# Three double-width projections, a list read later, and a program with two ends, in a hybrid encoder layer with mixture of experts

## The reference, cut to what matters

```python
proj = h @ w_in            # q 256 | k 256 | v 512 | og 512 | a1 16 | z 512 | xbc 1024 | dt 8
o_gla = rms_norm(gla_chunk_causal(q, k, v, log_a)) * silu(og)
y     = rms_norm((ssd_chunk_causal(xs, dt, a, bm, cm) + xs * ssd_d) * silu(z))
h = layer_norm(alpha * h + concat(o_gla, y) @ w_out)
top_v, top_i = lax.top_k(h @ router_w + router_b, 4); gates = softmax(top_v)   # of 32 experts
for each expert e, on the tokens that chose it:
    out += gate * ((min(a, 7) * sigmoid(1.702 * a) * (clip(u, -7, 7) + 1)) @ w_down[e] + b_down[e])
    # a = x @ w_gate[e] + b_gate[e],  u = x @ w_up[e] + b_up[e]
return layer_norm(alpha * h + out)
```

## Time and profile before

| what | value |
|---|---|
| median of three runs | 1058.77 us |
| the profiled execution | 1058.86 us |
| its span, first to last instruction | 1057.0 us |
| TensorE matmuls busy | 1021.6 us, 97% |
| TensorE weight loads busy | 449.5 us, 43% |
| VectorE, ScalarE, GpSimd busy | 228.6, 143.9, 29.7 us |
| moved by the DMAs | 426.21 MB, 403 GB/s over the span |

### The profile page before, as it was taken

How to read it: one execution, slowest core, us unless ns; L and a number is a source line. 1 busy time by engine, 2 the same in 40 slices (tenths; PEclk the granted TensorE clock), 3 DMA queues, 4 the chain that set the end, 5 groups by cost and what they waited for, 6 DMA issues and landing times.

```text
span 1057.0 us, 12137 instructions
## 1 busy us (share of the span) xinstructions
PE 1021.6 (97%) x5116; PEld 449.5 (43%) x5116; DVE 228.6 (22%) x495; ACT 143.9 (14%) x348; POOL 29.7 (3%) x50
## 2 busy tenths in 40 slices
PE   8999999999999999999999999999999999999997
PEld 7888764333333333333333333333333333333332
DVE  5453572111111111111111112211111111111112
ACT  3312331111111111011110111111111110011102
POOL 1230100000000000000000000000000000000000
PEclk9999999999999999999999999999999999999999
DMA  9894689999999999999999999999999999999995
GB/s 314 273 410 192 201 327 410 428 428 435 429 429 435 432 425 433 435 436 424 430 435 436 424 422 436 432 430 426 435 434 428 428 435 435 430 425 427 428 418 236
DMA packets 40011, 426.21 MB, mean 403 GB/s; under 512 B 6922, under 2 KB 19347, under 8 KB 23204
## 3 DMA queue, kind: packets, MB, share of 16 engines
q1 hardware_dynamic: 37940, 424.12, 95.6%
q10 hardware_dynamic: 2032, 1.53, 0.6%
HBM read 424.59 MB, written 1.05 MB: 403 GB/s over the span
## 4 chain that ended last, share of the span: by engine, by line
PE 72%; DMA 26%; ACT 1%; DVE 0%; issue 0%; SPq 0%; POOL 0%; DVEq 0%; POOLq 0%; ACTq 0%
PE bank L1200 30%; DMA ring<-in_moe_w_up 18%; PE bank L1251 15%; DMA ring<-in_moe_w_gate 8%; PE bank L1180 4%; PE bank L1172 4%; PE bank L856 3%; PE bank L871 2%; PE bank L1046 2%; PE bank L1034 1%; PE bank L988 1%; PE bank L1242 1%; PE bank L1120 1%; PE bank L949 1%; PE bank L1054 1%; PE bank L1220 1%
## 5 line engine op out<-in xcount | busy, mean ns | idle before, releaser
L1200 PE MATMUL bank<-ring,arena 128*64 128x512 f32 x1988 | 447.5, 603 | 23.8 <-DMA ring<-in_moe_w_up 20.3
L1200 PEld LDWEIGHTS bank<-ring,arena 128*64 128x64 f32 x1988 | 142.5, 139 | 298.7 <-issue 257.7
L1251 PE MATMUL bank<-ring,arena 128*64 128x512 f32 x1024 | 226.8, 595 | 1.5 <-issue 1.5
L1251 PEld LDWEIGHTS bank<-ring,arena 128*64 128x64 f32 x1024 | 71.5, 137 | 151.7 <-issue 150.2
L1641 DVE COPY arena<-bank 128x512 f32<-128x512 f32 x32 | 22.1, 692 | 326.0 <-PE bank L1251 326.0
L741 ACT ACTIVATE arena<-arena 128x512 f32<-128x512 f32 x32 | 20.1, 629 | 451.1 <-DVE arena L1628 451.1
L1180 PE MATMUL bank<-arena 64*128 64x512 f32 x256 | 72.0, 640 | 0.9 <-DVE arena L1641 0.9
L1172 PEld LDWEIGHTS bank<-arena 128*128 128x128 f32 x480 | 58.8, 196 | 22.8 <-issue 22.8
L1635 DVE TENSOR_SCALAR arena<-bank 128x512 f32<-128x512 f32 x32 | 22.1, 692 | 210.3 <-PE bank L1200 210.3
L752 ACT ACTIVATE arena<-bank 128x512 f32<-128x512 f32 x32 | 19.1, 597 | 337.4 <-PE bank L1242 337.4
L1172 PE MATMUL bank<-arena 128*128 128x128 f32 x480 | 64.5, 288 | 0.0
(11 more groups left out here) (281 smaller groups left out, 511.6 us busy)
## 6 DMA issues: line engine op xcount, KB each, us to landing
ring<-in_moe_w_down SPq DMA_DIRECT2D x25, 4096.0 KB, 29.6
ring<-in_moe_w_gate SPq DMA_DIRECT2D x24, 4096.0 KB, 25.4
ring<-in_moe_w_up SPq DMA_DIRECT2D x24, 4096.0 KB, 28.2
ring<-in_moe_w_gate SPq DMA_DIRECT2D x10, 2048.0 KB, 22.6
ring<-in_moe_w_up SPq DMA_DIRECT2D x10, 2048.0 KB, 15.2
ring<-in_moe_w_down SPq DMA_DIRECT2D x10, 2048.0 KB, 17.4
ring<-in_w_in SPq DMA_DIRECT2D x12, 1024.0 KB, 11.8
ring<-in_moe_w_gate SPq DMA_DIRECT2D x8, 1024.0 KB, 17.2
```

Source lines behind the costliest of these rows:

```text
L1200: ins = mm(b[h * SL:(h + 1) * SL, :], (xA[pp], xB)[q][:, k, par * SL:(par + 1) * SL], columns(unit_at(m, kt), h), start=False, stop=kt == ...
L1251: ins = mm(bank[6][h * SL:(h + 1) * SL, :], hidT[:, kt % 4, (kt // 4) * SL:(kt // 4 + 1) * SL], unit_at(2, kt)[:, h * 512:(h + 1) * 512], ...
```

## The change

1. The units of v, z and og (`WIDE`) become pairs: `w_wide(u)` is a unit of 512 columns. The same two DMAs are issued in the same places, but the first brings row groups 0 to 3 of all 512 columns and the second groups 4 to 7, in rows of 2 KB. `token_wide` makes eight products of 512 columns and waits for the second DMA ahead of the fifth. v: tile 0's first four stand ahead of the small sums, its other four behind them, and tile 1's eight behind D_ps. z: tile 0, then tile 1. og: tile 0, four of tile 1, the eight transposes, the other four.
2. `hidden_bias` of expert 0 moves from ahead of the first gathers to behind the last of them.
3. In tile 0, `counts` writes to bank 7, the gate transposes move to tile 3 (`BIASED`), and TensorE's wait for list_ok moves from ahead of the up product to ahead of the gather. VectorE's list work moves from ahead of its tile 0 to behind the first operation of it.
4. The second layer norm stands twice, in a block `If(nx < 1)` that waits for constants, and at the end of the block `If(nx > 0)`. TensorE's last four scatters move into the two blocks, behind its reading of nx. `link.steps` sets the count of an engine's own semaphore back between the two.

```diff
+def w_wide(n):
+    return ring[:, n // 4, (n % 4) * HW:(n % 4 + 2) * HW].rearrange("p (k n) -> p k n", k=KT)
 for n, c0 in enumerate(W_ORDER):
+    if n in WIDE or n - 1 in WIDE:
+        u = n if n in WIDE else n - 1
+        c0, rows = W_ORDER[u], HALVES[n - u]
+        sp.dma_start(w_wide(u)[:, rows, :], w_in[0, :, c0:c0 + 512].rearrange("(k p) n -> p k n", p=P)[:, rows, :]).then_inc(w_landed[n], 16)
...
+def token_wide(out, n, t, kts):
+    for kt in kts:
+        if kt % 4 == 0:
+            pe.wait_ge(w_landed[n + kt // 4], 16)
+        ins = mm(out, hT[:, kt, META + t * P:META + (t + 1) * P], w_wide(n)[:, kt, :], start=kt == 0, stop=kt == KT - 1)
+    return ins
...
-token_major(bank[5][:, 0:256], U_V, 0)
+token_wide(bank[5][:, :], U_V, 0, first_half)
 # dt sums
-token_major(bank[7][:, 0:256], U_V, 1)
+token_wide(bank[5][:, :], U_V, 0, second_half).then_inc(v_ps, 1)
 # la sums, D_ps
-for t, b in enumerate((bank[5], bank[7])):
-    token_major(b[:, 256:512], U_V + 1, t).then_inc(v_ps, 1)
+token_wide(bank[7][:, :], U_V, 1, range(KT)).then_inc(v_ps, 1)
...
+for t in range(NT):
+    token_wide(bank[(0, 5)[t]][:, :], U_Z, t, range(KT)).then_inc(z_ps, 1)
...
+token_wide(bank[6][:, :], U_OG, 0, range(KT)).then_inc(og_ps, 1)
+token_wide(bank[7][:, :], U_OG, 1, first_half)
+pe.wait_ge(mix_y, 2)
+mix_transposes(bank[0], z_t, (4, 5))
+mix_transposes(bank[5], z_t, (6, 7))
+token_wide(bank[7][:, :], U_OG, 1, second_half).then_inc(og_ps, 1)
...
 # TensorE, tile
 if first:
     counts()
+listing = isinstance(n, int) and n == BIASED
+if listing:
     gate_transposes()
...
-if first:
-    pe.wait_ge(list_ok, 1)
 hidden(1, bank[5], u_ok, u_ps)
...
+if first:
+    pe.wait_ge(list_ok, 1)
+if listing:
     pe.wait_ge(GT_ok, 1)
...
 # TensorE, the end
-for t in range(NT):
-    scatter(NE - 1, t, 1)
 pe.wait_ge(list_ok, 1)
 nx = pe.value_load(xcount[0:1, 0:1], min_val=0, max_val=MAXX)
+with pe.If(nx < 1):
+    last_scatters()
+    output_norm()
 with pe.If(nx > 0):
+    last_scatters()
     with pe.Fori(0, nx) as i:
...
+    output_norm()
 # ScalarE, the end (VectorE alike)
+with act.If(nx < 1):
+    output_norm(NE)
 with act.If(nx > 0):
...
+    output_norm(nx + NE)
```

More of the change, by code:

```diff
@@ L51 @@
 LATE = SPARED + 2
+BIASED = UNROLL - 1
 HALVES = (slice(0, 4), slice(4, 8))
@@ L336, in _ @@
             for n, c0 in enumerate(W_ORDER):
-                sp.dma_start(w_unit(n), w_in[0, :, c0:c0 + 256].rearrange("(k p) n -> p k n", p=P)).then_inc(w_landed[n], 16)
+                if n in WIDE or n - 1 in WIDE:
+                    u = n if n in WIDE else n - 1
+                    c0, rows = W_ORDER[u], HALVES[n - u]
+                    sp.dma_start(w_wide(u)[:, rows, :], w_in[0, :, c0:c0 + 512].rearrange("(k p) n -> p k n", p=P)[:, rows, :]).then_inc(
+                        w_landed[n], 16)
+                else:
+                    sp.dma_start(w_unit(n), w_in[0, :, c0:c0 + 256].rearrange("(k p) n -> p k n", p=P)).then_inc(w_landed[n], 16)
                 if n == 7:
@@ L741, in tile @@
                 nc.scalar.activation(s_c, a_c, ACT.Sigmoid, scale=SALPHA).then_inc(sig_ok, 1)
-                if first:
+                if isinstance(n, int) and n == BIASED:
                     act.wait_ge(GT_ps, 1)
@@ L771, in _ @@
                     tile(i + NE, 0, False, False, None, True)
-            nc.scalar.preload_act_table_set("natural_log_exp_and_others")
-            act.wait_ge(scat[1], nx + NE)
-            def mean_part(h):
-                return nc.scalar.activation(cg[h], bank[2 + h][:, :], ACT.Identity, scale=-1.0 / D, accum_out=sso[:, h:h + 1])
-            def square_part(h):
-                return nc.scalar.activation(cg[h], cg[h], ACT.Square, scale=-1.0 * D, bias=nmean[:, 0:1], accum_out=sso[:, 2 + h:3 + h])
[L781 to L793, removed]
+                output_norm(nx + NE)
         @block.tensor
@@ L884, in _ @@
             token_major(bank[4][:, 0:256], U_K, 0)
-            meta_rows(bank[1][:, 64:64 + HK], HK, [(U_K, g * HK) for g in range(4)])
+            meta_rows(bank[1][:, 64:64 + HK], HK, w_unit(U_K))
             pe.wait_ge(sT_ok, 1)
@@ L919, in _ @@
             ins.then_inc(D_ps, 1)
[L920 to L923 removed]
+            token_wide(bank[7][:, :], U_V, 1, range(KT)).then_inc(v_ps, 1)
+            meta_rows(bank[3][:, 0:HV], HV, w_wide(U_V)).then_inc(v_ps, 1)
             pe.wait_ge(wx_ok, 1)
@@ L1214, in tile @@
                     counts()
+                listing = isinstance(n, int) and n == BIASED
+                if listing:
                     gate_transposes()
-                else:
+                if not first:
                     pe.wait_ge(yd_ok, n)
@@ L1667, in _, with centred, output_norm @@
             nx = dve.value_load(xcount[0:1, 0:1], min_val=0, max_val=MAXX)
+            def centred(t, h, mean, op):
+                at = slice(h * 512, (h + 1) * 512)
+                return stt(z2[:, t, at], bank[2 * t + h][:, :], mean, lnbc[:, 0, at], op, ALU.mult)
+            def output_norm(scattered):
+                dve.wait_ge(ln2_in, 32)
+                dve.wait_ge(scat[0], scattered)
+                for h in range(2):
+                    ins = nc.vector.bn_stats(stats[:, h, :], bank[h][:, :])
+                link(ins)
+                link(nc.vector.bn_aggr(mv[:, 0, :], stats[:, 0:2, :]))
+                ts(vtmp[:, 0:1], mv[:, 0, 1:2], LN_EPS, None, ALU.add).then_inc(var2, 1)
+                for h in range(2):
+                    centred(0, h, mv[:, 0, 0:1], ALU.subtract).then_inc(cen, 1)
+                dve.wait_ge(nmean_ok, 2)
+                dve.wait_ge(scat[1], scattered)
+                for h in range(2):
+                    ins = centred(1, h, nmean[:, 0:1], ALU.add)
+                link(ins)
+                dve.wait_ge(rstd2, 1)
+                for h in range(2):
+                    at = slice(h * 512, (h + 1) * 512)
+                    stt(z2[:, 1, at], z2[:, 1, at], rstd[:, 1:2], lnbc[:, 1, at], ALU.mult, ALU.add).then_inc(fin, 1)
+            steps = link.steps[0]
+            with dve.If(nx < 1):
+                output_norm(NE)
+            link.steps[0] = steps
             with dve.If(nx > 0):
```

117 lines of the change are left out of this document (52 added, 65 removed).

## The result

The changed kernel took 1061.03 us (median of 16 runs, 1060.21 to 1061.9), the kernel before 1059.28 beside it: ratio 1.0018, 95% interval 1.0011 to 1.0025. Two of the 16 runs of the kernel before are stray ones, 2643.74 and 5250.7 us; without them its median is 1058.97. The changed kernel is slower by some 1.8 us; the prediction had 1058.0 and a range up to 1059.5. The profiled execution took 1060.52 us with a span of 1058.8 (before: 1058.86 and 1057.0).

What follows compares the result with a forecast made beforehand. The stream of expert weights on full DMA engines was taken as the bound, its start set by TensorE's chain. Terms -1.00 + 0.15 - 0.15 + 0 + 0.2 = -0.8 us gave 1058.0 us, range 1056.6 to 1059.5.

Steps and rivals of the forecast that it cites:

- the two ends: Last layer norm, standing twice: 0 for TensorE's reading and jump, +0.2 us for ScalarE's last test and jump, bounds 0.05 to 1.3.
- the jump at the end: Rival: ScalarE's jump behind the last landing must fetch its instructions, +1.7 us there, 1059.5 us in all; chance 0.12.
- The wide products: v, z and og projections: 96 records of 512 columns at 0.429 us replace 192, 42.22 to 41.22 us, -1.00 us.
- The bound that I set below, 0.2: Least saving in v, z and og, if a record of 512 columns cost twice one of z's, 0.438 us.
- The bias product: Expert 0's bias product moved behind the gathers: between 0 and 0.42 us later, taken as +0.15 us on every gate piece.
- The up pieces: Tile 0: up product starts 0.8 us sooner on top of the shift, worth 0.15 us, at most 0.3.
- the shift: Everything behind the projections comes sooner: 1.00 us from the wide products, less 0.15 for the bias product.
- starved stream: Rival: earlier up pieces fill the whole hole in the DMA rate behind 158 us, -1.9 us, 1056.9 us; chance 0.14.
- The front as a whole: Everything ahead of the ends: -1.00 wide products, +0.15 bias product, -0.15 up pieces.

Runs made afterwards that it cites:

- e2: The kernel before with part 4 alone, two ends on TensorE, ScalarE and VectorE: 1061.59 us, ratio 1.0024.
- e3: The kernel before with two ends on ScalarE alone: 1059.43 us, ratio 1.0004.
- e7: The kernel before with two ends on VectorE alone: 1059.60 us, ratio 1.0008.
- e4: The kernel before with two ends on TensorE alone: 1060.44 us, ratio 1.0014.
- e13: The changed kernel with each engine's second end cut to scatters and norm, overfull work left out, tests and jumps kept: 1058.84 us, ratio 1.0002.
- e12: The kernel before with part 3 alone (bias product, sums and list moved), old single ends: 1058.59 us, ratio 0.9998.
- e8: Changed front, single ends on ScalarE and VectorE; TensorE tests and jumps before its last four tiles, which stand in each branch: 1058.15 us, ratio 0.9994.
- e9: Changed front, old single ends, TensorE's overfull block, test and jump left out: 1058.42 us, ratio 0.9998.
- e10: As e9, with ScalarE's and VectorE's overfull blocks, tests and jumps left out too: 1058.05 us, ratio 0.9994.
- e15: e1 without the two gathers in TensorE's overfull block, 64 instructions that never run: 1058.63 us, ratio 0.9996.
- e17: The kernel before with the wide products and their loads alone, old single ends, two gathers left out of TensorE's overfull block: 1058.65 us, ratio 0.9993.
- e1: The changed kernel with parts 1 to 3 kept and the old single ends on all three engines: 1063.12 us, ratio 1.0039.
- e6: The kernel before with 15 never-run products (60 instructions) at the head of TensorE's overfull block: 1062.78 us, ratio 1.0037.
- e16: e1 with 16 products (64 instructions) that run, four in each of tiles 16 to 19: 1066.0 us, ratio 1.0059.
- e5: e1 with 48 never-run products (192 instructions) at the head of TensorE's overfull block: 1063.37 us, ratio 1.0042.
- e11: e1 with 48 products of 16 columns that run in one tile, under TensorE's wait for the stream: 1073.71 us, ratio 1.014.

## Why the prediction was wrong

**The step that failed is the two ends**: "I take 0.2, as the register is already read", with 0 for TensorE and no term for VectorE. Measured alone they cost 2.5 us (e2), in the changed kernel 2.2 between the last landing and the end. I had priced one jump, ScalarE's, since it is the last thing on the chain. That term was mis-sized, 0.6 us in the profile and 0.4 in the times (e3), and within its bounds. The missed ones are TensorE's and VectorE's. They come when these engines have done all their work, so I gave them no place on the path. But their fetches go by DMA just when the last output rows are issued and moved (1053.1 and 1054.7 us): VectorE's draws out the last issue (0.64 us in e7), and with TensorE's the rows land late (4.89 us behind the issue in e4 instead of 2.87). An engine that is done can still delay the end. That length is the cause e13 shows; that it acts by the fetches is argued, since they go together with the length, and how a packet draws out an issue or a landing is not shown.

I had also misread two rows. The 0.76 us of rest ahead of L1329, which I took for reading and jumping, stand ahead of L1336 in the changed kernel as well, where no jump lies between the scatters and the norm, so they are not its price. And the view of the earlier trace rows has a second packet, which I passed over:

```profile
q14 instruction: 1, 0.01, 0.7%
```

It starts at 1047.1 us in the kernel before and is gone from there in e7, so it was VectorE's. The trace showed that VectorE's jump fetches too, and I gave it no term.

**The rival "the jump at the end"** had the right side, at 1059.5 us, and packets like that of the earlier trace rows do come. It was wrong on the place. ScalarE's part was a third of what it gave, and its packet (1059.1 us, 1057.7 in e3) starts only behind the end of the span.

**The wide products**: forecast -1.00 us, in the chain -0.2 to -0.3. A record of 512 columns took the 0.43 us that I read from L1046. What was wrong is the other side. 7.10/32 and 14.01/64 are 0.219 to 0.222 us a record, but the records within follow each other every 0.2145 us, half of 0.429, and the rest, 0.24 to 0.28 us, is an edge that each group has once. The groups after have it too: 13.93 us is 32 x 0.429 and 0.2. L1046's 6.87, from which I took my price, had no edge. The bound that I set below, 0.2, was about the value.

**The bias product**: forecast +0.15, and the first gate piece came 0.09 us sooner where the releases ahead of it were 0.12 us sooner: +0.03.

**The up pieces**: forecast 0.8 us sooner on top of the shift of 0.85, 1.65 in all, and 0.15 worth. Measured 0.81 in all, 0.72 of it on top of a shift of 0.09 (0.72 in e12 too), and worth nothing that shows in e12. So this step was right to 0.1 us, and the shift was missing. The "starved stream" falls with it: the rate from 158 to 190 us didn't rise with them (388 to 382, 424 to 426 GB/s).

**The front as a whole**: forecast -1.0, measured -0.4 in the landing of the last weights, and 0.9993 to 0.9998 in the five kernels whose end doesn't spoil it (e8, e9, e10, e15, and e17 with the wide products alone), some 0.5 us. Each interval alone includes no change.

**What I had not thought of**: that the length of the code is part of the change. Parts 1 to 3 with the old ends would have been 4 us slower (e1), by place alone. In the changed kernel the two ends take away that standstill, since TensorE now reads nx ahead of the scatters and jumps over the long block only behind the norm, and put 2.2 us in its place. Judged against the kernel before they lose; against e1 they gain 2.

## What to carry to other kernels

Near the end of a program, where nothing covers it, count jumps and code as work: a jump over a long block costs even on an engine that is done, and a target shortly ahead of a border between two pieces of the code stalled TensorE for 2.3 us, beside which its clock went to the lower level. If a change adds or removes instructions and the time moves by a few microseconds that no work explains, look at the first instructions behind each late jump, and pad or shorten code that never runs. An average over a group of records is not the distance of two records; price a merger of instructions by the distance.

## What the runs showed of the hardware

- 60 never-executed instructions cost 4 us (e6), and 64 fewer gave back as much (e15 against e1). Some 2 us of this are the standstill; the rest goes with the clock, which was at 1.2 GHz beside its end for 3.4 us (e6) and 6.8 us (e1), and beside a slow jump for 6.8 us (e16) and 10.2 us (e5). A fall of 3.4 us without a standstill goes with 12.7 us from the last weights to the end (e10), against 11.4 without it (e9).
- TensorE's jump near the end took 0.35 us in the kernel before, e1, e6 and e15. It took 3.5 us where the block was 192 instructions longer (e5), 3.7 where all lay 64 further on (e16), 3.4 over the second block of the changed kernel and 6.8 amid the stream (e8).
- ScalarE sees the last rows landed 2.9 to 3.3 us behind the start of SyncE's last issue in the fifteen kernels in which neither TensorE nor VectorE jumps over a long block behind its last work (e13's blocks are short). With VectorE's jump it is 3.6 us (e7), with TensorE's 4.6 to 4.9 (changed kernel, e2, e4).
- 48 products of 16 columns in a row took 17.9 us (e11): one every 0.22 us for the first 2.9 us, at the upper clock, then one every 0.43 us at the lower. Five of 128 columns took 1.38 us at the upper (e15), 0.28 each. The narrow padding was cheaper only until the clock fell.
- The fastest kernels that do the whole work are e8 (1058.15 us) and the kernel before (1058.69 beside it), which these runs can't tell apart. Those with a part of the overfull block left out are no candidates, but e15 shows what a more compact block would give the changed front: 1058.6 us, which can't be told from the kernel before either.
